# VectorE's lo part of a weight chunk goes between the side step and the evacuation step, one chunk further ahead

## What is computed

```python
# twice (l = 0, 1)
u = rms_norm(x, norm_w) * (1.0 + scale) + shift
proj = jnp.dot(u, w_in)                       # 2048 x 19064, then split
y_fox = fox_attention(fq, fk, fv, log_f) * silu(fg)
y_dsa = dsa_attention(dq, dk, dv, iq, ik, iw) * silu(dg)   # scores of an index, top 64
xbc = silu(causal_depthwise_conv(sxbc, conv_w, conv_b))    # 3072 channels
y_ssd = rms_norm((ssd_scan(xs, dt, a, bs, cs) + d_skip * xs) * silu(sz), ssd_norm)
merged = g0 * (y_fox @ w_o_fox) + g1 * (y_dsa @ w_o_dsa) + g2 * (y_ssd @ w_o_ssd)
x = x + gate * (merged @ w_out)
# once
z = rms_norm(x) @ w_in_2                      # u_lru, g_lru, q, k, v, g_attn, m_lru, m_attn
h = rg_lru(conv(u_lru)) + reversed rg_lru(conv(u_lru))
merged = sigmoid(m_lru) * ((h * silu(g_lru)) @ w_proj_a) + sigmoid(m_attn) * ((attn * silu(g_attn)) @ w_proj_b)
x = x + rms_norm(merged @ w_out_2)
```

## Time and profile before

| what | value |
|---|---|
| median of 3 runs | 3430.95 us (3424.48 to 3431.2) |
| the profiled execution | 3426.33 us, of which the span of its instructions 3424.5 us |
| granted TensorE clock, mean | 0.986 of 2.4 GHz |
| PE, share of the span busy | 96% |
| DVE | 66% |
| ACT | 50% |
| HBM read | 710.08 MB, mean 210 GB/s |

### The profile page before, as it was taken

One profiled execution on the slowest core, in us unless ns is written; L12 is line 12 of the kernel. 1 busy time (PEld: TensorE's weight loads), 2 busy tenths in 40 slices (PEclk: granted clock), 3 DMA queues, 4 the chain that ended last, 5 costly groups with the idle time before them and its releaser, 6 DMA issues.

```text
span 3424.5 us, 43659 instructions
## 1 busy us (share of the span) xinstructions
PE 3300.5 (96%) x18122; PEld 2865.5 (84%) x18122; DVE 2245.1 (66%) x2695; ACT 1699.9 (50%) x2096; POOL 46.8 (1%) x90
## 2 busy tenths in 40 slices
PE   4899999999999999999999999999999999999998
PEld 3689979788888887898898878888898899988887
DVE  6778877866666556786666576655567776544454
ACT  4355664654443445556646544444447865434343
POOL 0000000000000000000000000000000000000000
PEclk8899999999999999999999999999999999999999
DMA  9754566567777555444444567765555443465553
GB/s 376 286 213 174 187 240 255 210 239 267 261 266 296 204 196 184 172 159 169 172 179 160 175 244 272 271 234 197 186 185 192 178 172 134 163 221 192 190 190 140
DMA packets 102917, 719.31 MB, mean 210 GB/s; under 512 B 12176, under 2 KB 12256, under 8 KB 18752
## 3 DMA queue, kind: packets, MB, share of 16 engines
q1 hardware_dynamic: 93888, 675.38, 53.6%
q0 software_dynamic: 8256, 37.64, 3.1%
q10 hardware_dynamic: 576, 3.50, 0.3%
HBM read 710.08 MB, written 6.40 MB: 209 GB/s over the span
## 4 chain that ended last, share of the span: by engine, by line
PE 87%; DVE 8%; ACT 3%; issue 1%; DMA 1%; DVEq 0%; ACTq 0%
PE G L1258 80%; DVE LL L1862 3%; PE BA L1406 1%; PE BD L1379 1%; PE BD L1441 1%; DVE S L2070 1%; DVE RAW L1873 1%; DMA KV<-in_x_dram 0%; ACT HH L1501 0%; PE BC L1392 0%; DVE RAW L1855 0%; DMA RAW<-in_w_ada_packed_dram 0%; PE BE L1324 0%; PE BA L1460 0%; PE BC L1460 0%
## 5 line engine op out<-in xcount | busy, mean ns | idle before, releaser
L1501 ACT ACTIVATE HH<-RAW 128x2048 fp32r<-128x2048 f32 x546 | 1044.8, 1914 | 1091.5 <-PE G L1258 1063.9
L1862 DVE TENSOR_TENSOR LL<-RAW,HH 128x2048 fp32r<-128x2048 f32 x546 | 1247.7, 2287 | 357.0 <-ACT HH L1501 356.6
L1258 PE MATMUL G<-HH,UH 128*128 128x512 f32 x2528 | 1005.7, 398 | 45.4 <-DVE LL L1862 40.5
L1258 PE MATMUL G<-LL,UH 128*128 128x512 f32 x2528 | 989.4, 391 | 0.0
L1258 PE MATMUL G<-HH,UL 128*128 128x512 f32 x2528 | 989.1, 391 | 0.0
L1258 PE MATMUL G<-UH,HH 128*128 128x256 f32 x2080 | 603.7, 290 | 11.6 <-DVE XS L2106 7.7
L1258 PEld LDWEIGHTS G<-HH,UH 128*128 128x128 f32 x2528 | 477.8, 189 | 149.8 <-DVE LL L1862 47.4
L1258 PE MATMUL G<-UH,LL 128*128 128x256 f32 x2080 | 589.7, 283 | 0.0
L1258 PE MATMUL G<-UL,HH 128*128 128x256 f32 x2080 | 589.6, 283 | 0.0
L1258 PEld LDWEIGHTS G<-LL,UH 128*128 128x128 f32 x2528 | 477.3, 189 | 101.4
L1258 PEld LDWEIGHTS G<-HH,UL 128*128 128x128 f32 x2528 | 477.9, 189 | 99.2 <-issue 2.6
(11 more groups left out here) (360 smaller groups left out, 2309.4 us busy)
## 6 DMA issues: line engine op xcount, KB each, us to landing
RAW<-in_w_in_packed_dram SPq DMA_DIRECT2D x402, 1024.0 KB, 4.8
RAW<-w_ada_turned_packed_dram SPq DMA_DIRECT2D x92, 1024.0 KB, 4.9
RAW<-in_w_out_packed_dram SPq DMA_DIRECT2D x48, 1024.0 KB, 4.8
RAW<-in_w_o_ssd_packed_dram SPq DMA_DIRECT2D x32, 1024.0 KB, 4.8
RAW<-in_w_o_fox_packed_dram SPq DMA_DIRECT2D x16, 1024.0 KB, 4.8
RAW<-in_w_o_dsa_packed_dram SPq DMA_DIRECT2D x16, 1024.0 KB, 4.8
RAW<-in_w_proj_a_packed_dram SPq DMA_DIRECT2D x16, 1024.0 KB, 4.8
RAW<-in_w_proj_b_packed_dram SPq DMA_DIRECT2D x16, 1024.0 KB, 4.8
```

Source lines behind the costliest of these rows:

```text
L1258: mm = pe.matmul(to, lt, rh, start=first, stop=end, skip_group_check=True)
L1501: a.activation(HH[g % NH][:, :n], RAW[buf(ch["f"])][:, :n], ACT.Copy).then_inc(*hi_done.up(g))
L1862: v.tensor_tensor(LL[buf(f)][:, :n], RAW[buf(f)][:, :n], HH[g % NH][:, :n].bitcast(F32), ALU.subtract).then_inc(*lo_done.up(g))
```

## The change

`lo` of a chunk was put at the start of the next `push`, after `hi` of the next chunk. Now `push` only notes the chunk in `self.low`, and `slot` puts its `lo` between the side step and the evacuation step. So `lo(g)` stands in the same push as `hi(g)`, ahead of that slot's evacuation step and not behind it.

```diff
     def slot(self):
         self.middle()
         self.side.step(self.plan)
+        self.lower()
         self.evac.step(self.plan)
+
+    def lower(self):
+        if self.low is not None:
+            self.put("lo", self.low)
+            self.low = None
...
     def push(self, ch):
+        self.lower()
         self.bring(ch)
-        if self.pend:
-            self.put("lo", self.pend[-1]["g"])
+        self.low = ch["g"]
         self.advance(1)
         self.pend.append(ch)
...
     def flush(self):
-        self.put("lo", self.pend[-1]["g"])
+        self.lower()
         self.advance(0)
...
         self.gemm(chunk(3, 0))
         self.slot()
+        self.low = chunk(3, 2)["g"]
         self.pend += [chunk(3, 1), chunk(3, 2)]
```

## The result

The changed kernel takes 3448.86 us, median of 4 runs (3448.54 to 3449.28), and the kernel before, run beside it, 3430.62 us (4 runs). The ratio is 1.0058 with a 95% interval of 1.0043 to 1.0073: slower by 18 us. The forecast was 3457 us and slower, with a range of 3430 to 3476. The profiled execution has a span of 3446.9 us against 3424.5 before, 22.4 us more, where the sum had 30. So the spans differ by more than the medians, and a difference of two spans is good to a few us only.

A forecast was written before the change was run, and what follows sets the result against it. PE, busy 96% of the span, was taken as the bound. Terms 17 + 4.7 + 13.6 + 5 - 11 + 0.6 made 30 us, giving 3456 from the profiled execution or 3461 from the median; forecast 3457 us, range 3430 to 3476.

The forecast's parts named there:

- What bounds the kernel: Whole kernel: PE is busy 96% of the span, so reordering can win little; 14.1 us of waiting on lo is left.
- Term A: First layer's convolution: taps, tanh, hi, relu, sums and lo become a single chain, making PE late; 17 us lost, ends 9 and 22.
- Term B: Second layer's convolution, last tiles: the chain of 7.1 us per push makes PE late; 4.7 us lost, ends 0 and 9.
- Term C: Six ends of sz blocks: sz_put waits behind the newest chunk's lo, delaying the gemm; 13.6 us lost, ends 8 and 18.
- Term D: Clock at the sz places: longer PE gaps bring half a fall on three of five; 5 us lost, ends 0 and 17.
- The rival of this case: The clock falls at each sz place, +17 us for D in place of 5; 3468 us, 14% chance.
- The rule: Trainium skill, clock gate: a transpose "doesn't count as PE-busy the same way", so the whole sz gap counts; D would be 17 us.
- Term E: Heads steps, 1960 to 1996 us and second convolution's start: lo no longer waits behind evacuation; -11 us, ends -6 and -14.
- losses and gains cancel: Rival: slack and lead leave A at most 9, B 0, C 8, against a gain of 14; 3430 us, 12% chance.
- The first rival: The lead is enough: in the index stage hi runs ahead of ACT's tanh, so no chain forms; 3412 us, 8% chance.

The follow-up runs named there:

- Undoing the seven tiles: The changed kernel with lo behind the evacuation step again only in the first layer's first seven convolution tiles, beside the index scores: 3438.09 us.
- both losing parts in the old order: The changed kernel with lo behind the evacuation step again at sz normalization and write-back and in all convolution steps: 3405.69 us, ratio 0.9937 to the kernel before.

## Why the prediction was right, and where it was off

**What bounds the kernel** held: a change of order moved less than 1%, and the losses are loops and single chains of waits, not work.

**Term A, 17 us.** Measured 16.3 by the lateness. The chain was right to a tenth: 8.8 us worked out, 8.85 in the timeline, 9.9 for the long sums, and 7.1 for the last tiles. The relu wait of 2 us is there. Undoing the seven tiles gave 10.6 (9 in the prediction), and what comes behind them is 5.7 (8 in the prediction). That hi must stand behind the tanh was shown by moving hi. What was wrong is the sign by which it would be seen: not waits of PE on lo, but on the product of the convolution (the row below has 237 to 470 us). I had followed lo to its gemm, and overlooked that the transposes stand ahead of that gemm in PE's order and wait for DVE's work behind lo.

```profile
PE BE L1360 <- DVE S L2087: 10.8, 13, 2.7
```

**Term B, 4.7 us.** Measured +7.1, inside the range of 0 to 9, but it isn't one thing. 4.4 us are waiting, mostly a single wait of a gemm for the product (the 3.6 us in the rows of the changed kernel above), and not a loss at each push: from 1510 to 1611 us the lateness stays at 14.7 us. The other 2.7 us are clock, which the term didn't hold: behind that wait, from 1625 us, the clock is at 1.2 GHz for 6.8 us.

**Term C, 13.6 us.** The six places give 1.2, 1.1, 2.9, 2.6, 2.6 and 2.9, 13.4 us in sum, and the wait on sz_put grew by 12.4 us. One more write-back at 661 us, without such a loop, cost 1.1, which the sum did not have.

**Term D, 5 us.** Measured 8.9. "Half a fall on three of the five" was the step that failed: all of the five gaps of 5.08 us with four transposes in them had a fall, four of them new. The price was the other error, in the opposite direction. I took 3.4 us from the earlier trace rows, but a stretch of 6.8 us at 1.2 GHz lies in part on the gap itself, and what gemms lose is 2.1 to 2.4 us. The rival of this case had it right that the clock falls at each place, and its 17 us were twice too many. The rule that it was the case of isn't shown by that: the four transposes take only 0.6 us of such a gap, and 30 of them kept the clock up. Nor were all the other five gaps of the kernel before 2 to 3 us long; the one near 676 us is 4.62, with matmuls of an attention step in it.

**Term E, -11 us.** This is the one term that was far off: 20.7 us with both losing parts in the old order, and as much in the changed kernel (-3.6, -5.3, -7.4 and -6.9 make 23.2). What I counted came: 6.3 for 5.2 near 1965 us, 3.2 for 3.3 near 1383, 2.1 for 1.6 near 1705, and in the changed kernel 1.8 for 1.2 at the start of the second convolution. Two places were left out. The first heads steps beside the scan gave 3.6: I had looked only at waits of PE on lo, and there it waits 1.0 us on lo and 1.6 us on the scan's weights, which DVE makes behind that lo. The rows of before, from 437 to 475 us:

```profile
PE BD L1441 <- DVE WW L2375: 1.6, 2, 0.8
PE G L1258 <- DVE LL L1862: 1.0, 1, 1.0
```

The other was the step at the earlier trace rows, near 1620 us. I had put its 5.14 us of idle time of DVE "inside term B", as if the loss of the convolution made it useless. It gave 5.5 us. Part of it is again a wait with another name, from 1600 to 1630 us:

```profile
PE BE L1324 <- DVE S L2027: 1.9, 1, 1.9
PE G L1258 <- DVE LL L1862: 1.5, 1, 1.5
```

and the clock, low for 3.4 us at 1624 us before, doesn't fall there.

**The sum.** 16.3 + 7.1 + 13.4 + 1.1 + 8.9 of losses, less 23.2 of gains and 1.3 in the opening, make 22.3 us, and the spans differ by 22.4. The prediction had 30, since its losses were 40 of the 47 measured and its gains 11 of 24. So the total is nearer than its terms: gains that were 13 us short and losses that were 7 short offset each other in part, and that is luck. By the medians the change costs 18.2 us, where the forecast of 3457 had 26. The rival *losses and gains cancel* had the gains too low as well (14), and 17 us of losses where 47 came. The first rival's condition was made true in the kernel with hi ahead of the convolution step. It took 3432.12 us and not 3412: the loss in the convolution went, but C, which the rival had paid back, stayed.

## What to carry to other kernels

Before an instruction is moved ahead of another on an in-order engine, ask at each place what it waits for itself: ahead of a step that waits for ACT's root it filled idle time (16 us won with the heads steps alone), and ahead of a step that feeds ACT it became a link of a loop through ACT (22 us lost) or of the chain to a write-back (20 us lost). A rule that holds everywhere in a plan is worth splitting by the step it passes. And gains are to be looked for under every name by which PE waits behind the moved instruction, not only under its own.

## What the hardware showed

Ten gaps between gemms in two kernels, each with four transposes in it, differ above all in their length. In the changed kernel there are five of 5.08 us. At four of them PE has 0.6 us of transposes at or near the start and then 4.1 or 4.6 us of nothing; at the one near 717 us the transposes stand between two waits of 2.15 and 2.27 us. After each of the five the granted clock was at 1.2 GHz for 6.8 us, and it began to fall before the gap was over: at 751.4 us, where the next gemm starts at 753.25. With the same five places at 3.22 or 2.63 us (sz in the old order), the stretches were 3.4 us long at three of 3.22 and absent at both of 2.63.

It is not the length alone. A gap of 5.08 us with the convolution in the old order, near 1872 us, had a stretch of only 3.4 us. A gap of 5.83 us near 690 us, with the matmuls of an attention step in it, had no fall in the changed kernel and one of 3.4 us in four of the others. And gaps of 2.46 us, at full clock in the kernel before, had a stretch of 3.4 us behind them near 1863 us with only the heads in the new order, and near 1906 and 1934 us with only the convolution in it. So a fall behind a short gap is a matter of the single execution too.

At 1.2 GHz a gemm's matmuls of 256 columns follow each other every 0.213 us, and at 2.4 GHz every 0.119. And f32 transposes, 30 of them in 3.44 us, kept the clock at 2.4 GHz in four gaps where the idle engine had lost it.
